# The last expert of layer 0 added by TensorE, the latents of layer 1 normed before its context, and layer 1's last slabs in halves

## The chip, the cores and the metric

The kernel runs on one core of a Trainium2 chip. A core has TensorE (PE, matrix products; its weight loads are shown apart as PEld), VectorE (DVE), ScalarE (ACT), GpSimd (POOL) and SyncE (SP), each with an order of its own; they meet through semaphores. Data lie in SBUF (128 partitions), products land in eight PSUM banks, and DMA queues carry data between HBM and SBUF. The metric is the device time of one execution in microseconds (us), the median of several; lower is better.

## The reference, cut to what matters

Two layers over 256 latent tokens and 256 context tokens of width 1024:

```python
for l in range(2):
    h = modulate(rms_norm(tokens, norm1_g[l]), shift, scale)          # latents and context, own modulation
    y = parallel_mixer(h, ...)                                        # one input projection; attention and HGRN2; output projection
    tokens = tokens + gate * y                                        # layer 1: latents only
    h2 = modulate(rms_norm(tokens, norm2_g[l]), shift2, scale2)
    tokens = tokens + gate2 * grouped_moe(h2, ...)                    # layer 1: latents only
return rms_norm(latents, final_g)

def grouped_moe(h, ...):                                              # 16 experts in 4 groups
    w = weights of the top 2 experts of the best group, per token
    return sum over e of w[:, e] * ((silu(h @ w_gate[e]) * (h @ w_up[e])) @ w_down[e])     # 1024 -> 512 -> 1024
```

All is float32, and a float32 product runs as two passes on PE, each with a record of its own in the trace (fp32r operands, split into a high and a low part, as one).

## The kernel before, in words

The token stream xT is kept with features on partitions: 8 feature tiles (KT) of 128, by 512 tokens; columns 0 to 255 are the context ("segment 0"), 256 to 511 the latents ("segment 1"). Weights stream through SBUF slabs of 2 MB. There is no scheduler: the order on each engine is the order of the code in that engine's block, and each engine waits on semaphores that count others' steps. So a step that stands early in an engine's block holds up all that is behind it there.

**Layer 0's experts** (dealt_experts). Every expert has 96 places, into which its tokens are dealt: 64 "near", 32 "rest". For each expert e, POOL gathers the rows of its tokens from token_table, PE turns them (L1185), and multiplies with gate and up: hidden_near (L1203, 64 places) and hidden_rest (L1214, 32). ACT applies silu, DVE multiplies into f_acts (L3101, L3109), PE turns it (turn_act, L1222), ACT copies f_turned, and PE multiplies with the down slab (down: L1232 near, L1239 rest). ACT copies the result to y_out, and SP stores it to expert_table in HBM (store_y, L1719 and L1721; the last expert's at L1768, its near half from ACT's queue). The hidden products of e + 1 stand before turn_act and down of e, which covers ACT and DVE. SP refills a slab when its products are over: gate and up at up_over, down (L1711) at down_over, in a fixed order per e, with the stores behind.

**join_tokens.** When all 16 experts are stored, POOL gathers for each of four blocks of 128 tokens the two rows of its two experts (tok_rows, L2512). ACT scales the first by its share (L2277), DVE adds the second times its share (L3129, "join"), PE turns the block (L1302), DVE adds it, times the modulation, to xT (L3137). Blocks 0 and 1 are context, 2 and 3 latents. PE multiplies ones meanwhile (L681, idle_products, read by nobody).

**Layer 1's first norm.** ACT squares xT (L2283), POOL adds squares of two tiles for six pairs (L2518), PE sums over features by one-column products (L1272), ACT takes the root (L2293), DVE its reciprocal, PE spreads it over partitions (L1285); DVE multiplies (normed, L2595, both segments at once), ACT modulates (hT, L1890, once per segment). normed has two buffers, so DVE waits for ACT's tile k - 2. Then PE makes the latents' queries (L823); ACT and DVE split hT into early_hi (L1943) and early_lo (L2637), the weights into near_hi (L1921) and ring_lo (L2655), and PE makes eight chunks of keys and gates for both segments, 24 passes each (L836, L840, L843).

**Layer 0's second norm** uses the same L2595 and L1890 ahead of the router.

**Layer 1's experts** (narrow_experts) take all 256 latents' chosen places, 64 per expert: gate L1472 and up L1473, turn L1485, down L1496, scatter of pairs of experts L1508 and L1512 (weights pair_hi and pair_lo, DVE, L3257 and L3267). SP loads each slab whole (L1641), in the order GATE e, UP e, DOWN e - 1, as slabs come free.

## Time and profile before

| what | us |
|---|---|
| median of three runs | 1462.76 (1461.70 to 1464.13) |
| profiled execution, its own time | 1461.11 |
| its span, first to last instruction | 1459.3 |
| PE busy / DVE / ACT / POOL in the span | 1400.1 / 694.5 / 527.2 / 157.1 |
| mean granted PE clock, share of full speed | 0.990 |
| last product of layer 0's experts to end of layer 1's first chunk | 836.7 to 894.2 |
| layer 0's second norm, first to last hT on ACT | 531.5 to 539.5 |
| layer 1's last expert, first gate product to the kernel's last product of experts | 1425.5 to 1449.7 |

Busy shares are averages over stages with different limits. What a stage is worth is read from what ends its waits last: a row of a timeline gives the start in us, the duration, engine and line, output and inputs, shapes, how many instructions were grouped, and in brackets how long the engine stood idle before and what released it. "issue" is a wait for nothing that the profile shows.

### The profile page before, as it was taken

What the parts mean: (1) busy time and instruction counts of PE and PEld (TensorE: products, weight loads), DVE (VectorE), ACT (ScalarE), POOL (GpSimd) and SP (SyncE); (2) the same over time, 40 slices, a digit from 0 to 9 for tenths busy, and PEclk for the clock granted to TensorE, in tenths of its full rate; (3) what the DMA queues carried; (4) which work ended last, traced back from release to release, by engine and by line L of the source; (5) the groups of instructions that cost most, each with busy time, mean ns of one, the idle gap of its engine ahead of it and who ended that gap; (6) DMA issues with size and microseconds to landing.
All of it is one profiled execution on the core that took longest, in us unless ns stands there. A gap on an engine that the chain in (4) does not pass through costs nothing. (4 is left out here: it accounts for less than half of the span.)

```text
span 1459.3 us, 20788 instructions
## 1 busy us (share of the span) xinstructions
PE 1400.1 (96%) x8454; PEld 899.4 (62%) x8454; DVE 694.5 (48%) x1201; ACT 527.2 (36%) x955; POOL 157.1 (11%) x163
## 2 busy tenths in 40 slices
PE   4999999999999999999999989999998998999997
PEld 2886667646888864444444378876856996344433
DVE  4477986475834442000000034976775774223223
ACT  5554452357233341111111136554346553112112
POOL 0007970000000001000000030074000000000000
PEclk9999999999999999999999979999999999999998
DMA  9762104671131758999999591120677756999993
GB/s 369 241 159 87 58 1 173 233 286 59 58 115 58 288 206 303 390 393 394 404 406 414 200 351 62 57 101 16 220 256 274 289 231 241 398 429 429 429 429 152
DMA packets 102952, 352.37 MB, mean 241 GB/s; under 512 B 23104, under 2 KB 26304, under 8 KB 88000
## 3 DMA queue, kind: packets, MB, share of 16 engines
q1 hardware_dynamic: 99136, 338.09, 60.4%
q0 software_dynamic: 2976, 10.49, 2.1%
q10 hardware_dynamic: 736, 2.36, 0.4%
q8 instruction: 71, 1.16, 0.3%
q14 instruction: 33, 0.27, 0.1%
HBM read 341.48 MB, written 13.63 MB: 243 GB/s over the span
## 5 line engine op out<-in xcount | busy, mean ns | idle before, releaser
L1472 PE MATMUL bank<-narrow_slab,picked 128*64 128x512 f32 x256 | 114.9, 602 | 3.7 <-issue 3.5
L1473 PE MATMUL bank<-narrow_slab,picked 128*64 128x512 f32 x256 | 115.0, 603 | 0.0
L1203 PE MATMUL bank<-slab,feed 128*64 128x512 f32 x512 | 113.4, 595 | 0.3 <-ACT feed L2227 0.3
L865 PE MATMUL bank<-hT,ring 128*128 128x512 f32 (+1 forms) x256 | 102.8, 539 | 0.0
L3101 DVE TENSOR_TENSOR f_acts<-bank,f_silu 64x512 f32<-64x512 f32 x16 | 11.1, 694 | 186.4 <-ACT f_silu L2233 186.4
L1203 PEld LDWEIGHTS bank<-slab,feed 128*64 128x64 f32 x512 | 35.8, 137 | 70.2 <-issue 70.2
L1472 PEld LDWEIGHTS bank<-narrow_slab,picked 128*64 128x64 f32 x256 | 34.1, 138 | 69.4 <-issue 68.0
L2500 POOL DMA_INDIRECT feed_rows<-token_table,slot_token x16 | 14.6, 913 | 551.5 <-DVE slot_token L3033 345.1
L3280 DVE TENSOR_TENSOR hidden<-bank,gated 64x512 f32<-64x512 f32 x16 | 17.4, 1085 | 109.4 <-ACT gated L2375 109.4
L865 PEld LDWEIGHTS bank<-hT,ring 128*128 128x128 f32 x256 | 45.9, 191 | 32.0 <-issue 30.6
L1232 PE MATMUL bank<-slab,f_turned 128*64 128x512 f32 x256 | 58.5, 598 | 0.6 <-issue 0.6
L1214 PE MATMUL bank<-slab,feed 128*32 128x256 f32 x1024 | 58.6, 380 | 0.0
L889 PEld LDWEIGHTS bank<-pair 128*128 128x128 f32 x384 | 47.1, 192 | 17.9 <-DVE pair L2739 11.2
L1496 PE MATMUL bank<-narrow_slab,hiddenT 128*64 128x512 f32 x256 | 57.8, 592 | 0.0
L2477 POOL TENSOR_TENSOR pair<-pf 128x512 f32<-128x512 f32 (+1 forms) x32 | 32.2, 1006 | 216.2 <-DVE pb L2702 205.8
L889 PE MATMUL bank<-pair 128*128 128x128 f32 x384 | 49.0, 277 | 3.0 <-DVE pair L2739 3.0
L2077 ACT ACTIVATE gsig<-bank 128x512 f32<-128x512 f32 (+1 forms) x32 | 15.8, 492 | 99.2 <-PE bank L1010 99.1
L2023 ACT ACTIVATE pair<-pair 128x1024 f32<-128x1024 f32 (+1 forms) x32 | 27.0, 843 | 59.8 <-POOL pair L2478 59.8
L2233 ACT ACTIVATE f_silu<-bank 64x512 f32<-64x512 f32 x16 | 9.5, 591 | 105.2 <-PE bank L1203 105.2
L2375 ACT ACTIVATE gated<-bank 64x512 f32<-64x512 f32 x16 | 9.4, 589 | 100.9 <-PE bank L1473 100.9
L1214 PEld LDWEIGHTS bank<-slab,feed 128*32 128x32 f32 x1024 | 31.6, 110 | 20.4
L2161 ACT ACTIVATE probs<-bank,narow 128x512 f32<-128x512 f32 (+1 forms) x48 | 29.4, 615 | 33.3 <-DVE narow L2892 33.2
(421 smaller groups left out, 3022.4 us busy)
## 6 DMA issues: line engine op xcount, KB each, us to landing
ring<-in_w_in SPq DMA_DIRECT2D x23, 2048.0 KB, 9.8
ring<-in_w_ada SPq DMA_DIRECT2D x16, 2048.0 KB, 11.2
slab<-in_w_gate SPq DMA_DIRECT2D x16, 2048.0 KB, 15.2
slab<-in_w_up SPq DMA_DIRECT2D x16, 2048.0 KB, 18.8
slab<-in_w_down SPq DMA_DIRECT2D x16, 2048.0 KB, 19.7
narrow_slab<-in_w_gate SPq DMA_DIRECT2D x16, 2048.0 KB, 15.3
narrow_slab<-in_w_up SPq DMA_DIRECT2D x15, 2048.0 KB, 20.8
narrow_slab<-in_w_down SPq DMA_DIRECT2D x15, 2048.0 KB, 24.3
```

What stands on the lines that cost most here:

```text
L865: mm = T.matmul(beside[0][:, a:TOK], w[:, k, c * P:(c + 1) * P], hT[:, k, a:TOK], start=(k == 0), stop=(k == KT - 1))
L889: mm = T.matmul(o[:, (2 * i + b) * P:(2 * i + b + 1) * P], left, right, start=True, stop=True)
L1203: mm = T.matmul(bank[e % 2][NEAR * kind:NEAR * (kind + 1), :], feed[e % 2][:, k, 0:NEAR], w[kind][:, k, :], start=(k == 0), stop=(k == KT ...
L1214: mm = T.matmul(bank[4][REST * c:REST * (c + 1), a:a + SEG], feed[e % 2][:, k, NEAR:DEALT], w[c // 2][:, k, c % 2 * SEG:(c % 2 + 1) * SEG] ...
L1232: mm = T.matmul(bank[6][NEAR * half:NEAR * (half + 1), :], f_turned[:, k * NEAR:(k + 1) * NEAR], w[:, k, half * 512:(half + 1) * 512], sta ...
L1472: T.matmul(bank[0][0:64, :], x, gate[:, k, :], start=(k == 0), stop=(k == KT - 1))
L1473: mm = T.matmul(bank[0][64:128, :], x, up[:, k, :], start=(k == 0), stop=(k == KT - 1))
L1496: mm = T.matmul(bank[3][64 * half:64 * half + 64, :], hiddenT[:, k, :], w[:, k, half * 512:(half + 1) * 512], start=(k == 0), stop=(k == 3))
L2023: S.activation(e[:, 0], e[:, 0], ACT.Exp)
L2161: S.activation(probs[at][:, 0:nk], result(("S", l, n))[:, 0:nk], ACT.Exp, bias=narow[:, at, 0:1], accum_out=narow[:, at, 1:2]).then_inc(se ...
L2477: G.tensor_tensor((stays, moves)[way][0], mid, left, ALU.subtract)
L3280: V.tensor_tensor(dealt(hidden[64:128, :], 4), in_turn(bank[0][64:128, :], 4), in_turn(gated[64:128, :], 4), ALU.mult) .then_inc(sem["hidd ...
```

## The change

- **Layer 0's last expert (15) is not stored and gathered.** After expert 4, DVE writes late_hot (hot_rows: for each token and place, the token's weight if it has that place at expert 15, 8 operations). PE turns it (turn_late), DVE copies it out as late_spread (2 copies). From y_out of expert 15, PE adds weights times rows straight into the banks that hold the turned rows (scatter_last): the latents into banks 0 to 3, later the context into banks 4 to 7. 8 products have 64 places on their rows, 8 have 32. The gathers cover experts 0 to 14, and wait for those alone; two small DVE operations zero the share of expert 15 in them.
- **Order.** Down of 14 stands ahead of hidden of 15. The latents' blocks 2 and 3 are joined first, turned around down_rest of 15, and added to xT by DVE (8 tiles), then the scattered 8 tiles once more. The context's blocks are turned by products with the identity (turn_joined) between the latents' squares, spread and norm; its squares are made by POOL (5 tiles) and DVE (3), and its norm follows the latents' one. hT, early_hi and early_lo are made per segment.
- **Down slabs.** At e = 12 SP loads DOWN 14 ahead of GATE 15 and UP 15. Layer 1's ring loads follow the gathers.
- **Layer 0's second norm.** ACT modulates the context, POOL the latents; the router's products wait for both.
- **Layer 1's last slabs.** GATE 15 and UP 15 are loaded in halves in turn, and PE waits for the first halves, then at k = 4 for the rest. The last pair_hi is made by ACT, and the table for the roots is loaded earlier.

Core of the diff:

```diff
+            def scatter_last(sg):
+
+                home = 0 if sg else 4
+                cols = slice(sg * SEG, (sg + 1) * SEG)
+                out = lambda d: bank[home + d // 2][:, d % 2 * SEG:(d % 2 + 1) * SEG]
+                pe.wait_ge(sem["late_kept"], 2)
+                pe.wait_ge(sem["y_kept"], 2 * N_EXPERTS - 1)
+                for d in range(4):
+                    for half in range(2):
+                        n = 4 * half + d
+                        if sg and d % 2 == 0:
+                            pe.wait_ge(sem["tok_added"], 2 * (n // 2) + 2)
+                        T.matmul(out(n), y_out[1][NEAR * half:NEAR * (half + 1), d * P:(d + 1) * P],
+                                 late_spread[NEAR * half:NEAR * (half + 1), 0, cols],
+                                 start=(sg == 1 and d % 2 == 0), stop=False)
+                pe.wait_ge(sem["y_kept"], 2 * N_EXPERTS)
+                for j in range(2):
+                    for c in range(4):
+                        mm = T.matmul(out(2 * c + j), y_out[1][REST * c:REST * (c + 1), 512 + j * P:512 + (j + 1) * P],
+                                      late_spread[REST * c:REST * (c + 1), 1, cols], start=False, stop=(j == 1))
+                        if j:
+                            mm.then_inc(sem["late_scattered"], 1)
...
+                    if k == 2:
+                        join_squares(0)
+                    if k == 3:
+                        spread_segment(0)
...
+                    def turn_late():
+
+                        pe.wait_ge(sem["row_of_ready"], 2)
+                        for part in range(2):
+                            pe.wait_ge(sem[("feed_high", "feed_low")[part]], N_EXPERTS)
+                            for t in range(4):
+                                mm = T.transpose(bank[2 + part][:, t * P:(t + 1) * P], late_hot[:, t, part, :], ident)
+                            mm.then_inc(sem["tok_turned"], 1)
+
+                    def latents_late():
+
+                        pe.wait_ge(sem["act_made"], 2 * N_EXPERTS)
+                        pe.wait_ge(sem["late_kept"], 2)
+                        for t in JOIN_ORDER[:2]:
+                            if t == JOIN_ORDER[1]:
+                                down_rest(LAST)
+                            pe.wait_ge(sem["tok_joined"], t - 1)
+                            for d in range(KT):
+                                c = d % 2 * SEG + t % 2 * P
+                                mm = T.transpose(bank[d // 2][:, c:c + P], tok_rows[0][:, t, d * P:(d + 1) * P], ident)
+                            mm.then_inc(sem["tok_turned"], 1)
+                        scatter_last(1)
...
+                    turn_act(LAST - 1)
+                    turn_late()
+                    down_near(LAST - 1)
+                    down_rest(LAST - 1)
+                    pe.wait_ge(sem["crowd_ready"], 1)
+                    crowded = pe.value_load(crowd_int[0:1, 0:1])
+                    hidden_near(LAST)
+                    hidden_rest(LAST)
+                    pe.wait_ge(sem["late_kept"], 2)
+                    idle_products(bank[3][:, 0:P], 4)
+                    turn_act(LAST)
+                    idle_products(bank[3][:, 0:P], 3)
+                    down_near(LAST)
+                    with pe.If(crowded > dealt_first[0]):
+                        latents_late()
...
-                    for t in range(4):
-                        if t:
-                            idle_products(bank[7][:, P:2 * P], 2)
-                        if t == 3:
-                            add_squares(0, range(2))
-                        pe.wait_ge(sem["tok_joined"], t + 1)
-                        for d in range(KT):
-                            c = d % 2 * SEG + t % 2 * P
-                            mm = T.transpose(bank[t // 2 * 4 + d // 2][:, c:c + P], tok_rows[0][:, t, d * P:(d + 1) * P], ident)
-                        mm.then_inc(sem["tok_turned"], 1)
...
+                    context_turned(3, 0)
+                    join_squares(1)
+                    context_turned(5, 1, range(4))
+                    spread_segment(1)
+                    context_turned(5, 1, range(4, KT))
+                    scatter_last(0)
...
+                        if e == LAST - 3:
+                            refill(e, DOWN, "down_over", 2 * e + 2)
...
+                        if late in HALVED and part == UP:
+                            e, kind = LATE_ORDER[m - 1 - len(FIRST)]
+                            name, k = spent_by[l][kind]
+                            sp.wait_ge(*total(2, None, name, e, k))
+                            for half in range(2):
+                                fill_first(m - 1, half)
+                                fill_first(m, half)
+                            continue
...
-                    pe.wait_ge(*total(1, None, "x_added", phases[1][1] - 1, 4))
-                    idle_products(bank[7][:, P:2 * P], 40)
-                    join_tokens()
...
-                    for sg in range(1 if lo else 0, 2):
+                    act.wait_ge(sem["normed_ready"], normed_before(count) + k + 1)
+                    for sg in range(1 if lo else 0, 1 if count == 1 else 2):
...
+                for k in range(KT):
+                    pool.wait_ge(sem["normed_ready"], KT + k + 1)
+                    G.tensor_scalar(hT[:, k, SEG:TOK], normed[:, k % 2, SEG:TOK], gain2[:, 0, k, 0:1], mod[:, 0, 3 * KT + k, 0:1],
+                                    ALU.mult, ALU.add).then_inc(sem["latents_modulated"], 1)
...
+                    def hot_rows():
+
+                        for t in range(4):
+                            for part, (first, size, copies) in enumerate(((0, NEAR, 2), (NEAR, REST, 4))):
+                                op = V.tensor_scalar(late_hot[:, t, part, :].rearrange("p (a n) -> p a n", a=copies),
+                                                     iota[:, first:first + size].unsqueeze(1).to_broadcast([P, copies, size]),
+                                                     place[:, t, LAST:N_EXPERTS], weight[:, t, LAST:N_EXPERTS],
+                                                     ALU.is_equal, ALU.mult)
+                        op.then_inc(sem["row_of_ready"], 1)
...
+                        for n, t in enumerate(JOIN_ORDER[:2]):
+                            join_rows(t, n)
+                        dve.wait_ge(sem["tok_turned"], 4)
+                        for d in range(KT):
+                            add_joined(1, d)
+                        join_rows(JOIN_ORDER[2], 2)
+                        for d in range(KT):
+                            dve.wait_ge(sem["late_scattered"], d // 2 + 1)
+                            add_joined(1, d)
...
-                        keep_high(None, N_EXPERTS - 2, 1, 1)
...
```

PE at the end of layer 0's experts, before: down of 14 (slab2), turn_act and down of 15 (slab4), then the branch that skips the overflow phase.

```order
L1232 MATMUL bank6<-slab2_248,f_turned_270 64x512 [waits y_kept,act_kept,slot_full2]
L1232 MATMUL bank6<-slab2_248,f_turned_270 64x512 x7
L1239 MATMUL bank7<-slab2_248,f_turned_270 32x256 [waits y_kept]
L1239 MATMUL bank7<-slab2_248,f_turned_270 32x256 x15
L1222 MATMUL bank5<-const_53,f_acts_269 128x64 [waits act_kept,act_made]
L1222 MATMUL bank5<-const_53,f_acts_269 128x64 x5
L1232 MATMUL bank6<-slab4_250,f_turned_270 64x512 [waits y_kept,act_kept,slot_full4]
L1232 MATMUL bank6<-slab4_250,f_turned_270 64x512 x7
L1239 MATMUL bank7<-slab4_250,f_turned_270 32x256 [waits y_kept]
L1239 MATMUL bank7<-slab4_250,f_turned_270 32x256 x15
L1571 TENSOR_LOAD crowd_int_69 [waits crowd_ready]
L1572 COMPARE_AND_BRANCH
```

The same place now, from turn_act of 14 on; late_hot are the weights' places, slab1 and slab3 up and gate of expert 15.

```order
L1311 MATMUL bank5<-const_53,f_acts_269 128x64 [waits act_kept,act_made]
L1311 MATMUL bank5<-const_53,f_acts_269 128x64 x5
L1342 MATMUL bank2<-const_53,late_hot_279 128x128 [waits feed_high,row_of_ready]
L1342 MATMUL bank2<-const_53,late_hot_279 128x128 x3
L1342 MATMUL bank3<-const_53,late_hot_279 128x128 [waits feed_low]
L1342 MATMUL bank3<-const_53,late_hot_279 128x128 x3
L1321 MATMUL bank6<-slab2_248,f_turned_270 64x512 [waits y_kept,act_kept,slot_full2]
L1321 MATMUL bank6<-slab2_248,f_turned_270 64x512 x7
L1332 MATMUL bank7<-slab2_248,f_turned_270 32x256 [waits y_kept,slot_full2]
L1332 MATMUL bank7<-slab2_248,f_turned_270 32x256 x15
L1375 TENSOR_LOAD crowd_int_69 [waits crowd_ready]
L1292 MATMUL bank1<-slab1_247,feed1_258 64x512 [waits act_made,feed_high,slot_full3,slot_full1]
```

Down of 14 moved ahead of hidden of 15, with turn_late and the register load; the branch comes behind down_near of 15.

ACT at the start of layer 1, before: squares, roots per segment, then hT of tile after tile for both segments.

```order
L2277 ACTIVATE tok_rows0_277<-tok_rows0_277,share_275 128x1024 [waits tok_there3]
L2283 ACTIVATE square_late_255<-xT_49 128x256 [waits tok_added] x12
L2293 ACTIVATE token_std_74<-bank0,epsv_72 128x2 [waits normed_ready,psum_ready]
L2283 ACTIVATE square_late_255<-xT_49 128x256 [waits tok_added] x4
L2293 ACTIVATE token_std_74<-bank1,epsv_72 128x2 [waits normed_ready,psum_ready]
L1890 ACTIVATE hT_50<-normed_119,mod_60,gain1_61 128x256 [waits normed_ready]
L1890 ACTIVATE hT_50<-normed_119,mod_60,gain1_61 128x256
```

And now, from the last of the scalings on.

```order
L2441 ACTIVATE tok_rows0_277<-tok_rows0_277,share_275 128x1024 [waits tok_there1]
L2435 ACTIVATE square_late_255<-xT_49 128x256 [waits tok_added] x8
L2018 ACTIVATE token_std_74<-bank0,epsv_72 128x2 [waits normed_ready,psum_ready]
L2000 ACTIVATE hT_50<-normed_119,mod_60,gain1_61 128x256 [waits normed_ready] x8
L2070 ACTIVATE early_hi_125<-hT_50 128x256 [waits h_ready] x8
L2037 ACTIVATE near_hi0_127<-ring_51 128x1024 [waits slot_full0]
L2037 ACTIVATE near_hi1_128<-ring_51 128x1024
L2018 ACTIVATE token_std_74<-bank0,epsv_72 128x2 [waits normed_ready,side_ready]
L2076 ACTIVATE hT_50<-normed_119,mod_60,gain1_61 128x256 [waits normed_ready]
L2079 ACTIVATE early_hi_125<-hT_50 128x256 [waits h_ready]
```

Squares, root and hT of the latents moved ahead of everything of the context, whose squares left ACT; the context's root stands behind early_hi and near_hi.

SP's last expert loads of layer 1, before; narrow_slab8 and 6 take GATE 15 and UP 15.

```order
L1641 DMA narrow_slab5_242<-in_w_down 128x4096 [waits halves_done]
L1641 DMA narrow_slab8_245<-in_w_gate 128x4096 [waits hidden_done]
L1641 DMA narrow_slab6_243<-in_w_up 128x4096 [waits hidden_done]
L1641 DMA narrow_slab7_244<-in_w_down 128x4096 [waits halves_done]
L1641 DMA narrow_slab0_237<-in_w_down 128x4096 [waits hidden_done]
```

And now, where 128x2048 is half a slab.

```order
L1738 DMA narrow_slab5_242<-in_w_down 128x4096 [waits halves_done]
L1738 DMA narrow_slab8_245<-in_w_gate 128x2048 [waits hidden_done]
L1738 DMA narrow_slab6_243<-in_w_up 128x2048
L1738 DMA narrow_slab8_245<-in_w_gate 128x2048
L1738 DMA narrow_slab6_243<-in_w_up 128x2048
L1738 DMA narrow_slab7_244<-in_w_down 128x4096 [waits halves_done]
L1738 DMA narrow_slab0_237<-in_w_down 128x4096 [waits hidden_done]
```

The whole loads of GATE 15 and UP 15 became four halves in turn; the down loads behind them stay.

## Rows read from the trace of the kernel before

**Rows 1.** Timeline of PE, 834 to 895: start, us, engine, line, operation, shapes, count, idle before.

```profile
834.81 1.93 PE L1239 MATMUL bank<-slab,f_turned 128*32 128x256 f32 x32
840.68 11.67 PE L681 MATMUL bank<-const 128*128 128x128 f32 x80 [3.93 <-issue]
...
860.83 0.58 PE L1272 MATMUL bank<-const,square_late 128*128 128x1 f32 x4 [1.69 <-POOL square_late L2518]
861.26 1.07 PE L1302 MATMUL bank<-const,tok_rows 128*128 128x128 f32 x8
...
864.65 5.25 PE L1272 MATMUL bank<-const,square_late 128*128 128x1 f32 x24 [0.26 <-POOL square_late L2518]
...
874.57 14.08 PE L823 MATMUL bank<-hT,ring 128*128 128x256 f32 x64 [0.70 <-ACT hT L1890]
...
892.16 2.02 PE L843 MATMUL bank<-early_hi,ring_lo 128*128 128x512 f32 x8
```

**Rows 2.** Timelines of SP, POOL, ACT and DVE around the same place.

```profile
837.22 1.94 SPq L1768 DMA_DIRECT2D expert_table<-y_out  x4
...
841.67 0.95 POOL L2512 DMA_INDIRECT tok_rows<-expert_table,row_of  x1 [67.18 <-issue]
...
850.17 1.15 ACT L2277 ACTIVATE tok_rows<-tok_rows,share 128x1024 f32<-128x1024 f32 x1 [12.98 <-DMA tok_rows<-expert_table,row_of]
...
873.43 7.97 ACT L1890 ACTIVATE hT<-normed,mod,gain 128x256 f32<-128x256 f32 x16 [3.23 <-DVE normed L2595]
881.30 4.25 ACT L1943 ACTIVATE early_hi<-hT 128x512 fp32r<-128x512 f32 x8
885.46 1.99 ACT L1921 ACTIVATE near_hi<-ring 128x1024 fp32r<-128x1024 f32 x2
...
821.20 0.69 DVE L3101 TENSOR_TENSOR f_acts<-bank,f_silu 64x512 f32<-64x512 f32 x1 [12.45 <-ACT f_silu L2233]
...
858.82 1.28 DVE L3129 SCALAR_TENSOR_TENSOR tok_rows<-tok_rows,share,tok_rows 128x1024 f32<-128x1024 f32 x1
...
862.37 3.23 DVE L3137 SCALAR_TENSOR_TENSOR xT<-bank,mod,xT 128x256 f32<-128x256 f32 x8 [0.31 <-PE bank L1302]
```

**Rows 3.** Windows: length, busy time of PE, PEld, DVE, ACT, POOL, granted clock, DMA, GB/s.

```profile
864.00:873.00 9.00, 8.74 (x40) 8.59 (x41) 2.13 (x8) 2.31 (x8) 1.23 (x2) 0.50 1.05 388
```

**Rows 4.** Timeline of ACT in layer 0's second norm.

```profile
531.52 7.97 ACT L1890 ACTIVATE hT<-normed,mod,gain 128x256 f32<-128x256 f32 x16 [2.18 <-DVE normed L2595]
```

**Rows 5.** Timeline of PE, layer 1's last expert.

```profile
1425.49 0.61 PE L1472 MATMUL bank<-narrow_slab,picked 128*64 128x512 f32 x1 [2.62 <-issue]
...
1426.54 1.06 PE L1472 MATMUL bank<-narrow_slab,picked 128*64 128x512 f32 x1
...
1434.08 3.63 PE L1496 MATMUL bank<-narrow_slab,hiddenT 128*64 128x512 f32 x16
...
1447.84 1.06 PE L1508 MATMUL bank<-pair_hi,spread 128*128 128x256 f32 x4
```

**Rows 6.** Timeline of SP's queue, the loads of UP 15, DOWN 14 and DOWN 15.

```profile
1393.47 0.43 SPq L1641 DMA_DIRECT2D narrow_slab<-in_w_up  x1
1396.54 8.87 SPq L1641 DMA_DIRECT2D narrow_slab<-in_w_down  x2
```

**Rows 7.** DMA issues of 1393 to 1396 and 1396 to 1404: size, us to landing.

```profile
narrow_slab<-in_w_up SPq DMA_DIRECT2D x1, 2048.0 KB, 31.8
...
narrow_slab<-in_w_down SPq DMA_DIRECT2D x1, 2048.0 KB, 33.6
```

**Rows 8.** Timeline of PE in layer 0's attention: products with 64 rows.

```profile
300.72 0.70 PE L955 MATMUL bank<-nak,naq 64*128 64x256 f32 x4
```

**Rows 9.** Timeline of POOL, the pairs of squares.

```profile
859.48 1.20 POOL L2518 TENSOR_TENSOR square_late<-square_late 128x256 f32<-128x256 f32 x1 [7.88 <-ACT square_late L2283]
861.02 2.29 POOL L2518 TENSOR_TENSOR square_late<-square_late 128x256 f32<-128x256 f32 x3 [0.34 <-ACT square_late L2283]
```

**Rows 10.** The page's DMA issues: stores of y by SP, median us to landing.

```profile
expert_table<-y_out SPq DMA_DIRECT2D x30, 128.0 KB, 16.1
```

566 lines of the change are left out of this document (354 added, 212 removed).

## The prediction

> **What bounds the kernel now.** TensorE (PE) is the busiest engine by far, so I looked for the stretches in which it stands or runs work that nobody reads: first its timeline, then at each gap the engine that released it, then the windows with the granted clock.
>
> Three stretches bear on this change. The **seam** between layer 0's experts and layer 1 [rows 1]: the last expert's last product ends at 834.81 + 1.93 = 836.74; then 3.93 us of nothing, 11.67 us of filler products (L681), and the first chunk of layer 1's keys ends at 892.16 + 2.02 = 894.18. That is 57.4 us, of which only the queries (L823, 14.08 us) and one chunk (about 5.9 us) are large PE work. Its chain runs over the others [rows 2]: the stores of the last y (837.22, 1.94), the first gather on POOL at 841.67, its rows at ACT at 850.17, that is 8.5 us later, joins of 1.28 us and adds of 3.23 / 8 = 0.40 us on DVE. Then come squares, norm, and both segments' 16 hT on ACT (7.97 us). The clock falls in it [rows 3]: granted 0.50 (the 1.2 GHz level) in 864 to 873, where PE does little but one-column products (L1272).
>
> Second, **layer 0's second norm** goes at ACT's pace [rows 4]: 16 in 7.97 us, 0.996 us for each of 8 feature tiles. Third, **layer 1's last expert** waits 2.62 us, to 1425.49, for its weights [rows 5]: UP 15 is issued at 1393.47 [rows 6] and lands 31.8 us later, at 1425.3, and DOWN 14 lands at 1396.54 + 33.6 = 1430.1 [rows 7].
>
> **The seam, step by step.** Times are those of the clock of before; first with PE at the upper level.
>
> 1. Down of expert 14 now stands ahead of hidden of 15. Beside the same products PE gets 8 turnings of the weights' places (8 turnings take 0.95 us, 861.26 to 862.17 without its drain) [rows 1], a register load (1.0) and some 1.4 us of fillers while ACT and DVE make the last activations, which down of 14 covered before. So the last down_near ends near 838.1, where it ended at 834.8. The load and the branch lay in the 3.93 us of idle time of before, together with eight semaphore steps [rows 1]; bounds for both together are 0 and 3.9 us. I take 2.0, half, since the steps are gone from this place; 0.4 would gain 1.6 us, 3.9 lose 1.9.
> 2. Branch (to 839.1), turnings of block 2, down_rest, turnings of block 3: 842.9.
> 3. Gathers no longer wait for the last expert. y of 14 is kept by 820.8, stored by 822.8; with the 2.5 us that lay between the end of the stores and the first gather (839.16 to 841.67) POOL starts at 825.3, and with 8.5 us ACT gets rows at 833.8. Blocks 2 and 3 are joined near 839 [rows 2]. PE wants them at 839.1 and 841.9: about 3 us of slack for the second.
> 4. DVE adds the latents (8 of 0.40, to 846.2). PE scatters the last expert from y itself: 16 products, 32 passes, 8 products with 64 rows and 8 with 32. Four 64-row passes of 256 columns take 0.70 us with their drain [rows 8]; full passes take 14.08 / 64 = 0.22 each, 0.88 for four [rows 1]. So two run side by side (0.11 each) with some 0.2 on top, and I let four do so for 32 rows: 16 x 0.11 + 16 x 0.055 + 2 x 0.2 = 3.0 us. Bounds 2.6 (no change) and 32 x 0.22 = 7.0 (nothing side by side). I take 3.0, the row being of the same form. Latents complete: 851.2.
> 5. Context block 0 is turned by products (16 passes of 0.12: 2.1 us, where transposes took 0.95). The latents' squares on PE are 32 one-column passes: 7.0 us by the 0.22 of the lower level (5.25 / 24); at the upper one between 0.43 / 4 = 0.11 and 0.145 [rows 1], I take 4.3. Squares end at 855.3, std, reciprocal and spread at 856.9, first hT near 857.9, where the first of before is at 873.43 [rows 2].
> 6. PE turns the rest of the context, scatters it (3.0), starts queries: 863.7. The context's squares, another 4.3 us, end at 868.1. ACT is behind them in its own queue: 8 hT, spaced by DVE's context adds between them (864.6), 8 early_hi of about 0.33 (half the columns of a row of 0.53), two near_hi of 1.0 [rows 2], so the context's std stands at 869.2, its spread at 870.
> 7. DVE norms the context, per tile 0.41 + 0.35 + 0.35 (halves of rows of 0.69 and 0.61) and one ring_lo of 1.2: 879. Remaining passes of the first chunk: 883.8.
>
> So 894.2 - 883.8 = **10.4 us** at the upper level. Against that stands the clock: steps 5 to 7 hold two runs of one-column products and a thin stretch, 875 to 880, the kind in which it fell before [rows 3]. Low through the first squares alone costs 3.0 by the same steps, low through both 7.1, low from 851 to 882 12.3. I take 3.4, nearest to the first, because before both runs stood next to each other and here turnings, scatter and queries lie between. Seam: **10.4 - 3.4 = 7.0**.
>
> **Ports on POOL.** POOL's square at 859.48 took 1.20 us while DVE's join (858.82 to 860.10, both inputs in SBUF) ran, and three later ones 2.29, 0.76 each, beside adds whose second input is PSUM [rows 2, 9]. The Trainium skill's page "SBUF — State Buffer", section "Who interferes with whom", says that a DVE instruction with two SBUF inputs and a GpSimd one that reads SBUF shut each other out, and one with a single SBUF input doesn't. The rows agree; by it the second norm's DVE (one input in PSUM) is undisturbed, while POOL's five context squares may meet DVE's three: 0.8 to 1.6 us on a step that ends 1.1 before ACT is ready, so 0.5 us at most.
>
> **Second norm of layer 0.** POOL takes the latents' half. ACT's 0.5 and DVE's 0.69 per tile remain; POOL's one-input operation has no row, its two-input one 0.76 to 1.20 [rows 9]. Pace 0.8 instead of 0.996: 8 x 0.19 = **1.5** gained; at 0.69 it is 2.4, at 1.20 a loss of 1.6. I take 0.8, a little over the undisturbed row.
>
> **Tail.** GATE and UP of 15 come in interleaved halves. 2 MB take 1430.1 - 1425.3 = 4.8 us, so both first halves lie there at 1420.5, both wholes at 1425.3. Hidden can start where its wait began, 1422.9, and needs the second halves half of its 7.0 us later, at 1426.4. Without the wait its passes should not stretch to 1.06 either, as those after 1426.54 did, and it ends near 1430. Down of 14 then waits for DOWN 14, 1430.1, and starts there instead of 1434.08 [rows 5, 7]: **3.9**. Two bounds: 2 (the halves' smaller pieces land late), 4.2. pair_hi moved to ACT counts nothing: PE's products follow one another at 1447.84 without a wait [rows 5].
>
> **At no cost.** The 8 hot-row operations and two copies lie in DVE's 12.45 us of waiting per expert [rows 2]; without it they would cost some 3 us. DOWN 14 first on SP pushes GATE 15 and UP 15 back by one slab, 4.8 us, while hidden of 15 itself moves back by the down and the turnings of step 1, over 6 us; without that cover it costs the difference. Layer 1's first ring load moves from 839 to 842, and is needed at 861.
>
> **Sum.** 7.0 + 1.5 + 3.9 = 12.4 us. The profiled execution took 1461.11, so 1448.7; the median of before is 1.65 above it: **1450.4 us**.
>
> On the scatter, the Trainium skill ("TensorEngine Tiling (Array Packing)", "Key Properties" and "Theoretical Speedup") gives up to two times for 64 rows and four for 32, and a drain at each change of mode. Without drains this estimate is 2.6 us instead of 3.0, 0.7 us for both scatters.
>
> **Rivals.** (a) The clock stays at 1.2 GHz from the first squares to the end of the context's norm. For it: before, it came back only after 873, with dense work [rows 3]; against: queries and scatter between. 12.3 for 3.4: 12.4 - 8.9 = 3.5, **1459.3**. (b) The gathers start late. The stores of 14 lie behind DOWN 15 on SP's queue; the median of the y stores in the loaded stage is 16.1 us [rows 10]. Landing 9.2 us later costs 9.2 less the slack, 6.6: **1457.0**. Against: DOWN 15 should be through by 823. (c) The halves bring nothing, because the four pieces land together: 12.4 - 3.9 = 8.5, **1454.3**. (d) Slower: in the scatters nothing runs side by side, since all 32 passes add to few banks, and the clock falls with them: 32 x 0.43 = 13.8 us each, twice, and low until 882. By the steps the chunk then ends at 907.2, the seam loses 13.0, and 1.5 + 3.9 - 13.0 = -7.6: **1470.4**. It decides once a scatter exceeds about 9 us. (e) The new order doesn't do what it says: PE reaches the same places at the same time, because DVE's double adds (16 x 0.40 and a join) and ACT's queue take what the gathers gave: about **1462.8**.
>
> **Chances.** As summed 0.59, its own range 1446 (the clock never falls, 3.4 better, and POOL at its best, 0.9) to 1455; (a) 0.12, (b) 0.08, (c) 0.10, (d) 0.08, (e) 0.03. A measurement of this kernel can tell about 0.2%, 2.9 us, from no change. Within that, 1459.8 to 1465.7, lie (e) and under half of (a): 0.08; slower is (d), 0.08; faster 0.84. The range leaves out (d), (e), the upper half of (a) and the low tail: 1445 to 1459.5.
>
> **What would show it.** Right: rows at ACT before 836; the latents' first hT near 858; the first chunk's end between 882 and 890; hidden of 15 at 1422.9; a norm-2 pace of 0.8. Wrong: granted clock 0.50 beyond 860; a scatter over 5 us; the wait before block 2's turnings over 3 us; a wait for DOWN 14 past 1431.

## The result, and the profile after

The changed kernel took 1449.35 us (median of five, 1448.36 to 1453.55) against 1462.61 for the kernel before: ratio 0.9913, 95% interval 0.9898 to 0.9929. Forecast were 1450.4 and a range of 1445 to 1459.5. The span went from 1459.3 to 1446.7 us. Line numbers from here on are those of the changed kernel.

The seam, in the timeline of PE (start, us, engine, line, operation, shapes, count, idle before), answers to [rows 1]:

```profile
811.62 1.09 PE L1342 MATMUL bank<-const,late_hot 128*128 128x128 f32 x8
812.64 3.65 PE L1321 MATMUL bank<-slab,f_turned 128*64 128x512 f32 x16
...
831.16 3.66 PE L1321 MATMUL bank<-slab,f_turned 128*64 128x512 f32 x16
837.04 1.06 PE L1355 MATMUL bank<-const,tok_rows 128*128 128x128 f32 x8 [2.22 <-issue]
838.03 1.94 PE L1332 MATMUL bank<-slab,f_turned 128*32 128x256 f32 x32
839.90 1.09 PE L1355 MATMUL bank<-const,tok_rows 128*128 128x128 f32 x8
842.05 0.67 PE L821 MATMUL bank<-late_spread,y_out 64*128 64x256 f32 x2 [1.06 <-DVE xT L2785]
843.53 1.99 PE L821 MATMUL bank<-late_spread,y_out 64*128 64x256 f32 x14 [0.81 <-DVE xT L2785]
...
848.87 3.63 PE L849 MATMUL bank<-const,square_late 128*128 128x1 f32 x32
852.36 1.55 PE L806 MATMUL bank<-const,tok_rows 128*128 128x128 f32 x8
...
856.39 2.00 PE L821 MATMUL bank<-late_spread,y_out 64*128 64x256 f32 x16
858.32 1.15 PE L827 MATMUL bank<-late_spread,y_out 32*128 32x256 f32 x16
859.40 5.45 PE L881 MATMUL bank<-hT,ring 128*128 128x256 f32 x24
864.68 3.63 PE L849 MATMUL bank<-const,square_late 128*128 128x1 f32 x32
...
880.01 0.50 PE L923 MATMUL bank<-early_hi,near_hi 128*128 128x512 f32 x1 [0.44 <-ACT early_hi L2079]
...
884.05 1.98 PE L923 MATMUL bank<-early_hi,near_hi 128*128 128x512 f32 x8
```

Where 3.93 us of standing and 11.67 us of fillers were, PE now stands 2.22 us, waits twice more for DVE (1.06 and 0.81 us), and otherwise has something to multiply. The second chunk starts at 884.05, where it was 894.03.

The other engines there (SP, POOL, ACT, DVE), for [rows 2]:

```profile
819.42 1.87 SPq L1868 DMA_DIRECT2D expert_table<-y_out  x4
...
826.62 0.95 POOL L2660 DMA_INDIRECT tok_rows<-expert_table,row_of  x1 [54.48 <-issue]
...
833.49 1.15 ACT L2441 ACTIVATE tok_rows<-tok_rows,share 128x1024 f32<-128x1024 f32 x1 [2.60 <-DMA tok_rows<-expert_table,row_of]
...
868.35 0.26 ACT L2018 ACTIVATE token_std<-bank,epsv 128x2 f32<-128x2 f32 x1 [0.90 <-PE bank L849]
...
834.68 1.28 DVE L2779 SCALAR_TENSOR_TENSOR tok_rows<-tok_rows,share,tok_rows 128x1024 f32<-128x1024 f32 x1 [5.01 <-ACT tok_rows L2441]
```

The gathers start at 826.62, 13 us before PE's last down_rest ends (838.03 + 1.94 = 839.97), not after it. The row at 868.35 matters below: ACT waits 0.90 us for PE's context squares. The last row is the join of block 2, done at 835.96, 1.1 us before PE turns it.

Windows of the same place (length, busy PE, PEld, DVE, ACT, POOL, granted clock, DMA, GB/s), for [rows 3]:

```profile
846.00:852.00 6.00, 5.59 (x57) 5.22 (x50) 4.51 (x9) 3.16 (x8) 0.00 (x0) 1.00 1.05 396
852.00:858.00 6.00, 6.00 (x39) 5.64 (x40) 1.76 (x5) 2.45 (x5) 0.00 (x0) 0.72 1.05 387
858.00:864.00 6.00, 6.00 (x41) 4.82 (x38) 4.51 (x13) 3.30 (x8) 3.06 (x5) 1.00 1.05 387
```

The second norm, ACT, POOL and DVE, for [rows 4], and the tail on PE, for [rows 5]:

```profile
531.63 1.20 ACT L2000 ACTIVATE hT<-normed,mod,gain 128x256 f32<-128x256 f32 x2 [2.18 <-DVE normed L2746]
533.08 1.20 ACT L2000 ACTIVATE hT<-normed,mod,gain 128x256 f32<-128x256 f32 x2 [0.25 <-DVE normed L2746]
...
531.70 1.15 POOL L2640 TENSOR_SCALAR hT<-normed,gain,mod 128x256 f32<-128x256 f32 x2 [324.45 <-DVE normed L2746]
...
532.36 1.29 DVE L2746 TENSOR_TENSOR normed<-xT,bank 128x512 f32<-128x512 f32 x2 [0.17 <-POOL hT L2640]
```

```profile
1412.85 0.64 PE L1579 MATMUL bank<-narrow_slab,picked 128*64 128x512 f32 x1
...
1420.26 3.65 PE L1603 MATMUL bank<-narrow_slab,hiddenT 128*64 128x512 f32 x16 [0.33 <-DMA narrow_slab<-in_w_down]
...
1437.06 3.43 PE L692 MATMUL bank<-const 128*128 128x256 f32 x8 [1.27 <-PEq L487]
1440.33 1.91 PE L1704 MATMUL bank<-const,y_rows 128*128 128x128 f32 x16
```

ACT starts two tiles each 533.08 - 531.63 = 1.45 us, so one each 0.72, and POOL needs 1.15 / 2 = 0.58. The last expert's hidden products follow without a wait, and down of 14 waits 0.33 us for its slab. The last two rows show something not foreseen: eight filler passes before the last turnings took 3.43 us; they took 1.97 before.

So I cut each trace at the same instructions. In us:

| stage, from and to | before | after | again (e12) | e5: norm and halves alone | e13: seam alone |
|---|---|---|---|---|---|
| norm: first normed to the first turning of hT behind the router's products | 9.73 | 7.38 | 7.39 | 7.40 | 9.72 |
| experts of layer 0, to the end of down 13 | 272.93 | 272.82 | 273.95 | 274.01 | 273.01 |
| seam, to the second chunk of layer 1 | 80.58 | 72.95 | 75.60 | 80.73 | 78.50 |
| on to down of 13, layer 1 | 523.69 | 523.71 | 522.76 | 522.40 | 524.74 |
| tail, down 13 to down 14 | 16.36 | 12.50 | 12.52 | 12.49 | 16.34 |
| end, down 14 to the last turnings | 18.83 | 20.07 | 17.71 | 18.00 | 18.68 |

Each stage begins where the one above it ends. The norm (-2.35) repeats: 7.37 to 7.40 us in every trace in which POOL modulates. So does the tail (-3.86): 12.40 to 12.53 us in every trace with halves. The seam does not: 7.6 us gained in one execution, 5.0 in another.

### The profile page after: what moved, and what is told of

It reads as the page before. It is cut to its first block and busy times, and to the rows that moved or that the text cites. A ratio compares the mean times of both kernels' runs of the same rounds, so it can differ in the third digit from the quotient of the medians.

```text
span 1446.7 us, 20895 instructions
## 1 busy us (share of the span) xinstructions
PE 1394.5 (96%) x8480; PEld 894.3 (62%) x8480; DVE 702.9 (49%) x1238; ACT 524.4 (36%) x949; POOL 160.3 (11%) x170
## 5 line engine op out<-in xcount | busy, mean ns | idle before, releaser
L1579 PE MATMUL bank<-narrow_slab,picked 128*64 128x512 f32 x256 | 113.3, 595 | 1.2 <-issue 0.9
L1580 PE MATMUL bank<-narrow_slab,picked 128*64 128x512 f32 x256 | 113.3, 596 | 0.0
L1603 PEld LDWEIGHTS bank<-narrow_slab,hiddenT 128*64 128x64 f32 x256 | 18.4, 137 | 36.7 <-issue 35.5
```

The lines of the kernel that those rows point to most:

```text
L1579: T.matmul(bank[0][0:64, :], x, gate[:, k, :], start=(k == 0), stop=(k == KT - 1))
L1580: mm = T.matmul(bank[0][64:128, :], x, up[:, k, :], start=(k == 0), stop=(k == KT - 1))
L1603: mm = T.matmul(bank[3][64 * half:64 * half + 64, :], hiddenT[:, k, :], w[:, k, half * 512:(half + 1) * 512], start=(k == 0), stop=(k == 3))
```

## The experiments

Each is the changed kernel with one edit, unless it says otherwise. Ratios are to the kernel before on the same chip. The changed kernel has 0.9913 in its first runs, and 0.9915 in a second set (e12) beside e6, e11 and e13; on the chips of the other experiments it wasn't run.

**The parts.** First the halves:

```diff
-    HALVED = (N_EXPERTS - 1,)
+    HALVED = ()
```

> The changed kernel with GATE and UP of layer 1's last expert loaded whole again, gate first; all else stays. My theory: the halves alone carry the tail's gain, so down of expert 14 in layer 1 starts 3.8 us later against the issue of its slab than in the changed kernel, and the run takes about 1453 us if the rest follows, or 1452 if the fillers before the last turnings run faster, as they did in the kernel before (1.97 us for 8 passes, 3.43 in the changed kernel). Rival: the tail was gained because the seam moved everything 10 us earlier against the queue; then the time stays at 1449.4.

Measured 1454.53 us, 0.9948 (0.9930 to 0.9966). PE's rows around the last expert:

```profile
1414.43 0.46 PE L1592 MATMUL bank<-const,hidden 64*128 64x64 f32 x4
1417.46 1.09 PE L1579 MATMUL bank<-narrow_slab,picked 128*64 128x512 f32 x1 [2.57 <-issue]
```

The wait of 2.57 us is back, the first pass takes 1.09, and from down 13 to down 14 it is 17.47 us, 5.0 more than with halves. The halves carry the tail; the rival is out. The 17.47 is also 1.1 more than before the change (16.36): the granted clock was 0.57 over 1416 to 1424 here, and 0.57 over 1426 to 1430 only in the kernel before.

The norm:

```diff
-                    for sg in range(1 if lo else 0, 1 if count == 1 else 2):
+                    for sg in range(1 if lo else 0, 2):
...
-                    G.tensor_scalar(hT[:, k, SEG:TOK], normed[:, k % 2, SEG:TOK], gain2[:, 0, k, 0:1], mod[:, 0, 3 * KT + k, 0:1],
-                                    ALU.mult, ALU.add).then_inc(sem["latents_modulated"], 1)
```

> The changed kernel with layer 0's second norm modulated by ACT alone, both segments, as before; POOL's eight operations are gone. Theory: the norm's pace goes from 0.72 us per tile back to 0.98 and the time rises by 2.3 to 2.5 us, to about 1451.8. Rival: the norm's gain is given back further on (slabs of the first experts land no earlier), then the first expert's products start at the same time and the run stays at 1449.4.

Measured 1456.11 us, 0.9954 (0.9937 to 0.9972). The stage took 9.73 us again, 2.35 more. The time rose by more than that, with a wide spread (1448.4 to 1459.0); in the profiled execution the seam took 76.15 us and the experts 274.21, 3.2 and 1.4 more than in the first trace of the changed kernel. Those two also differ between executions of one kernel (e12), so only the 2.35 is put down to the edit. What the rest of the rise is stays open: the expectation of 1451.8 was missed, and the ten times were spread over more than 10 us.

The order of the down slabs:

```diff
-                        if e == LAST - 3:
-                            refill(e, DOWN, "down_over", 2 * e + 2)
...
-                            if e != LAST - 3:
-                                refill(e, DOWN, "down_over", 2 * e + 2)
+                            refill(e, DOWN, "down_over", 2 * e + 2)
```

> The changed kernel with the down slab of expert 14 loaded behind GATE 15 and UP 15 again. In the changed kernel its first product runs at 812.64. Theory: the slab then lands some 9 us later than now, near 814 to 816, and PE waits 1 to 3 us in front of down of 14: 1450.5 to 1452. Rival: it lands in time anyway, since in the kernel before it landed at 816.0, 2.35 us of which are gone with the second norm, that is 813.7: 1 us at most, within what can be told from 1449.4.

Measured 1451.34 us, 0.9936 (0.9914 to 0.9958), and no wait in front of down of 14:

```profile
811.70 1.09 PE L1342 MATMUL bank<-const,late_hot 128*128 128x128 f32 x8
812.72 3.65 PE L1321 MATMUL bank<-slab,f_turned 128*64 128x512 f32 x16
```

The rival holds: the slab is there anyway, and this part of the change does nothing that can be measured in the time. It does move something: with the old order the first gather began 2.9 us after the last store was issued (820.90 to 823.79), against 5.3 in the changed kernel's first trace. The block then lay joined at 833.33, and PE still turned it at 837.97, behind a standing of 3.06 us. So gathers earlier than the changed kernel's gained nothing in this trace.

Norm and halves put into the kernel before (the same two edits, the other way round):

> The kernel before with two parts of the change alone: POOL modulates the latents in layer 0's second norm, and GATE and UP of layer 1's last expert come in halves. The seam stays as it was. Theory: 2.4 us from the norm and 3.8 from the tail, less at most 1.4 where the fillers before the last turnings run at 1.2 GHz, so 4.8 to 6.2 us under the kernel before; what is left to the changed kernel, 6.5 to 8 us, is the seam's. Rival: the seam gives less than it seems and these two carry nearly all: 9 us or more under the kernel before.

Measured 1455.21 us, 0.9951 (0.9936 to 0.9966): some 6.2 us under the kernel before, the upper end of what was expected, with the seam at its old 80.7 us.

The seam alone (e1's and e2's edits together):

> The changed kernel with the other two parts undone: ACT alone modulates layer 0's second norm, GATE and UP of layer 1's last expert come whole. What is left of the change is the seam (last expert added by PE, latents first) and the order of the down slabs. Theory: the parts add up, so the seam alone lies 5 to 7.6 us under the kernel before, where norm and halves alone lay 6.2 under it. Rival: the parts help each other, and the seam alone gives under 4 us.

Measured 1456.75 us, 0.9958 (0.9940 to 0.9976), 6.3 us under the kernel before. 0.9951 and 0.9958 leave 0.9909 if the parts add up, and the changed kernel has 0.9913. Within the intervals they do. Taken out one at a time they fit less well: the ratio rises by 0.0035 without the halves (e1), by 0.0041 without the norm (e2), and by only 0.0045 without both (e13). The difference, 0.0031, is about what the intervals of the four allow together, so whether the parts help each other a little stays open. The profiled execution of e13 had a long seam (78.50; a standing of 3.25 us before block 2 and four stretches at the lower clock).

**What the seam's gain hangs on.** One wait more on POOL before the gathers:

```diff
+                pool.wait_ge(sem["act_kept"], N_EXPERTS)
                 for t in JOIN_ORDER:
```

> The changed kernel with one wait more on POOL: the first gather also waits for the last expert's turned activations (830.9 in the changed kernel's trace, where the gathers begin at 826.6). Theory: the early gathers bring the seam's gain and have about 1 us of slack (joined 839.3, PE there at 839.9), so the blocks are joined 4.3 us later and the time rises by 3 to 4 us, to 1452.5 to 1453.5. Rival: the seam's end is set by PE's own work and the split norm, and 4 us are taken up by waits on the way (1.06 and 0.81 us before the scatter): under 2 us.

Measured 1456.39 us, 0.9967 (0.9952 to 0.9983). The first gather began 20.4 us after the turning of the weights' places (15.0 in the changed kernel). The join of block 2 on DVE, and then PE, show what that cost:

```profile
842.44 1.29 DVE L2780 SCALAR_TENSOR_TENSOR tok_rows<-tok_rows,share,tok_rows 128x1024 f32<-128x1024 f32 x1 [11.00 <-ACT tok_rows L2441]
...
843.88 1.94 PE L1355 MATMUL bank<-const,tok_rows 128*128 128x128 f32 x8 [7.28 <-DVE tok_rows L2780]
845.75 3.16 PE L1332 MATMUL bank<-slab,f_turned 128*32 128x256 f32 x32
```

```profile
837.00:844.00 7.00, 0.12 (x1) 0.15 (x2) 1.29 (x1) 1.43 (x2) 4.89 (x6) 0.82 0.93 325
844.00:849.00 5.00, 5.00 (x41) 2.89 (x42) 1.28 (x1) 2.51 (x4) 0.00 (x0) 0.57 0.77 307
```

Counted from that turning, the gathers were 5.4 us later. Their rows took 0.6 us longer to come, so block 2 was joined 6.0 us later, at 843.73. The slack of 1.1 us was there and took up its part: PE waited 5.1 us more. Then came a clock of 0.57, at which eight turnings take 1.94 instead of 1.06 and down_rest 3.16 instead of 1.94. The seam took 80.1 us, as long as before the change. Against the seam of e12 (75.6) that is 4.5 us more, near the 3 to 4 expected; against the first trace 7.1. The times rose by some 7 us, twice what was expected; one trace doesn't settle why.

So the seam's gain hangs on the early gathers: with them 5.4 us later the kernel took 1456.39 us, and on the same chip norm and halves without any of the seam took 1455.21. It isn't shown what the other pieces of the seam (the latents first, the context's norm behind theirs) give by themselves, since no run takes out one of them alone.

**Who ends the first chunk.** The context's spread ahead of the fourth query tile:

```diff
                     if k == 2:
                         join_squares(0)
-                    if k == 3:
                         spread_segment(0)
```

> The changed kernel with the context's spread put right behind its squares on PE, ahead of the fourth of the latents' query tiles (in the changed kernel it stands 1.8 us behind them, 0.9 us after its reciprocal). Theory now: PE itself is the bound of this stretch, since the queries took 1.76 us per tile and not the 0.88 that the prediction put in; the chain of the context's norm starts 1.1 us earlier but PE waits about 0.65 for it, so under 0.5 us changes. Rival, the prediction's step 7: the norm's chain over DVE and ACT is the bound, and the first chunk ends 1.1 us earlier, counted from the start of the squares.

Measured 1449.78 us, 0.9911 (0.9888 to 0.9933): no change. From the start of the context's squares to the second chunk it is 20.61 us; in e12, on the same chip and with the same stretches at the lower clock, 20.62. PE's rows:

```profile
867.76 3.63 PE L849 MATMUL bank<-const,square_late 128*128 128x1 f32 x32
872.03 0.73 PE L859 MATMUL bank<-const,token_rstd 128*128 128x128 f32 x4 [0.64 <-DVE token_rstd L2812]
872.55 10.48 PE L881 MATMUL bank<-hT,ring 128*128 128x256 f32 x40
882.68 2.17 PE L922 MATMUL bank<-early_hi,near_hi 128*128 128x512 f32 x8
```

PE now waits 0.64 us for the reciprocal, and then never again: the 0.45 us that it waited for early_hi in e12 are gone. What the chain gains PE gives back. This stretch is bound by PE and by the chain almost alike.

**The standing behind down_near.** The branch moved ahead of the last turn_act, inside both of its arms:

```diff
+                        pe.wait_ge(sem["late_kept"], 2)
+                        turn_act(LAST)
+                        idle_products(bank[3][:, 0:P], 3)
+                        down_near(LAST)
...
-                    pe.wait_ge(sem["late_kept"], 2)
-                    idle_products(bank[3][:, 0:P], 4)
-                    turn_act(LAST)
-                    idle_products(bank[3][:, 0:P], 3)
-                    down_near(LAST)
                     with pe.If(crowded > dealt_first[0]):
                         latents_late()
```

> The changed kernel with PE's branch moved ahead of the last turn_act, into the place of the first four fillers (1.16 us there, 2.22 us of standing behind down_near in the changed kernel). Theory: the branch's 2.2 us lie in part beside ACT's and DVE's work on the last activations, PE turns block 2 about 1.1 us earlier, and then block 3 waits for its join (839.3): 0.5 to 1 us less, 1448.4 to 1448.9. Rival: the standing is not the branch's but the wait for the joined block 2, and stays behind down_near: no change.

Measured 1450.83 us, 0.9918 (0.9894 to 0.9942): no change.

```profile
832.67 0.87 PE L1311 MATMUL bank<-const,f_acts 64*128 64x64 f32 x6 [3.63 <-issue]
833.47 1.65 PE L692 MATMUL bank<-const 128*128 128x128 f32 x6
835.05 5.76 PE L1321 MATMUL bank<-slab,f_turned 128*64 128x512 f32 x16
840.74 1.09 PE L1358 MATMUL bank<-const,tok_rows 128*128 128x128 f32 x8
```

The standing went with the branch, so it is the branch's and not a wait for block 2. (e3 says the same: there block 2 was joined 4.6 us before PE turned it, and PE still stood 3.06 us.) But it grew to 3.63 us, and behind it the granted clock was 0.60 over 833 to 841, so the last down took 5.76 us instead of 3.66. Whether the fillers ahead of it had kept the clock up isn't told apart from the standing itself.

**The clock.** Two filler products among the latents' squares:

```diff
                 for k in range(KT):
+                    if sg == 1 and k in (4, 6):
+                        idle_products(bank[1][:, 0:SEG], 1)
```

> The changed kernel with two filler products of 256 columns among the latents' 32 one-column passes (0.9 us more for PE). In the changed kernel the granted clock is 1.00 up to 852, 0.72 over 852 to 858, and the context's second turning and the spread take 1.7 us more than at the upper level. Theory: it is the one-column stretch that lets the clock fall; with the fillers it stays at 1.00 and PE reaches the queries some 0.8 us earlier, 1448.5. Rival: the clock falls here whatever PE runs (it also fell at other places in other executions), and the fillers cost their 0.9 us: 1450.2.

Measured 1453.34 us, 0.9938 (0.9914 to 0.9963).

```profile
852.00:858.00 6.00, 6.00 (x39) 5.90 (x39) 1.53 (x3) 0.80 (x3) 0.00 (x0) 0.75 1.05 388
858.00:864.00 6.00, 6.00 (x44) 4.87 (x43) 1.59 (x4) 2.18 (x4) 0.00 (x0) 0.68 1.05 386
```

The clock fell in the same place and stayed down longer. So these two fillers don't hold it, and the theory's forecast is out. That the one-column passes have nothing to do with the fall isn't shown by this: the clock fell at the end of the latents' squares in all twelve traces of kernels with the new seam, this one included. The rival says nothing about why it was worse than 0.9 us, but the trace does in part. The clock was low for longer behind the context's squares too:

```profile
868.00:874.00 6.00, 6.00 (x41) 5.82 (x40) 3.09 (x9) 4.35 (x11) 0.26 (x1) 0.84 0.02 4
874.00:880.00 6.00, 6.00 (x20) 4.97 (x20) 1.78 (x6) 1.30 (x4) 0.00 (x0) 0.59 0.00 0
```

In e12 below it was back at 1.00 by 877. The seam took 79.34 us here, 3.7 more than in e12. Why both stretches were longer isn't shown.

No fillers before the last turnings:

```diff
-                idle_products(bank[0][:, 0:SEG], 4)
                 for b in range(4):
                     pe.wait_ge(sem["early_rows"], b // 2 + 1)
```

> The changed kernel without the four filler products ahead of the last turnings of the output rows. In the changed kernel they ran at 1.2 GHz, 3.43 us instead of 1.97, and ended 1.4 us after the first rows were there. Theory: the fillers themselves hold the end, and without them the turnings start 1.4 to 2 us earlier but run at the lower clock (16 transposes in about 3.6 us instead of 1.91), so that 0 to 1 us is left: 1448.4 to 1449.4. Rival: the turnings wait for DVE and ACT rows piece by piece, the lower clock costs them nothing, and the whole 1.3 us shows: 1448.1.

Measured 1450.22 us, 0.9921 (0.9901 to 0.9941).

```profile
1441.35 3.65 PE L1703 MATMUL bank<-const,y_rows 128*128 128x128 f32 x16 [2.53 <-DVE y_rows L3605]
```

The turnings start when their rows are there, and take 3.65 us at the lower clock. From the start of the last scatter's last row to their end it is 7.2 us, against 7.5 with fillers at the lower clock and 5.7 (e3) with fillers at the upper one. The theory held in this: little or nothing is to be had. Its forecast of 0 to 1 us less isn't told apart from no change.

Fillers in the waits of the last scatter (two products of 256 columns, one before pair_hi, one before pair_lo):

```diff
+                            if last and half == 0:
+                                idle_products(bank[1][:, 0:SEG], 1)
                             pe.wait_ge(*total(ph, i, "hi_kept", e, half + 1))
...
+                            if last and half == 0:
+                                idle_products(bank[1][:, 0:SEG], 1)
                             pe.wait_ge(*total(ph, i, "lo_kept", e, half + 1))
```

> The changed kernel with two filler products of 256 columns (0.9 us of PE) in the waits of the last scatter, 1.45 and 0.71 us in the changed kernel. There the clock fell to 0.50 over 1434 to 1438 and the last scatter's and filler passes took 3.2 us more than in executions in which it did not. Theory: PE's waits let the clock fall here, and with fillers in them it stays: 1.3 us less where it fell, nothing elsewhere. Rival: as with the fillers among the squares, it falls or not whatever stands there: no change, or 0.3 us more.

Measured 1450.60 us, 0.9914 (0.9889 to 0.9939). In its trace the clock was 1.00 from the tail to the end of the last turnings. It was so too in that of the unchanged kernel beside it (e12), so the trace can't tell the two apart; the time says no change.

The changed kernel once more:

> The changed kernel as it is, beside the three others on their chip. Theory: the places at which the clock falls differ from execution to execution of one kernel, so the stretch from the turning of the weights' places to the second chunk differs by 1 to 4 us from the 72.4 of the changed kernel's first trace, and the time lies at 1449 to 1451. Rival: the falls stand at fixed instructions, and the stages repeat within 0.3 us.

Measured 1450.44 us, 0.9915 (0.9892 to 0.9938). Windows of its seam:

```profile
844.00:849.00 5.00, 4.19 (x24) 2.88 (x26) 2.98 (x6) 1.15 (x1) 0.00 (x0) 0.66 0.72 239
849.00:855.00 6.00, 5.59 (x60) 5.21 (x52) 4.51 (x9) 3.16 (x8) 0.00 (x0) 1.00 1.06 392
855.00:859.00 4.00, 4.00 (x23) 4.00 (x23) 0.42 (x2) 0.26 (x1) 0.00 (x0) 0.57 1.05 387
...
873.00:877.00 4.00, 4.00 (x15) 3.41 (x15) 1.82 (x6) 1.45 (x3) 0.00 (x0) 0.66 0.00 0
```

Three falls, at the latents' scatter, behind the latents' squares and behind the context's; the first trace had the second alone. The same instructions take 2.65 us more. In nine executions (the first trace, e1 to e4, e6, e11 to e13; e3 moves one load and e6 one spread, the others leave this stage as the change has it) it took 72.95 to 78.50 us, 75.6 in the middle. Read in steps of 1 us, the granted clock goes with the length:

| stretches below full clock in the seam | seam, us |
|---|---|
| one | first trace 72.95 |
| two | e1 74.20, e4 74.73, e3 74.89 |
| three | e12 75.60, e6 75.74, e11 75.90, e2 76.15 |
| four | e13 78.50 |

So each costs about 1.4 us, an estimate from 72.95 with one and 75.6 to 76.2 with three. The fall at the end of the latents' squares is in all nine, one behind the context's in six; the others lie between the branch and the end of the latents' scatter, at different places. Both theory and rival are right in part: one fall stands at fixed instructions, the others don't. No version was found that beats the changed kernel.

## Why the prediction was right, and where it was not

**The sum** said 12.4 us; 13.3 were measured between the medians, 12.6 between the spans, and 12.6 between the medians of e12's set (1463.03 and 1450.44). That it came so near is in part luck: the first trace's seam is the shortest of nine, with the fewest stretches at the lower clock, and errors of both signs stand in the sum. Its three terms came out as follows.

**Seam: 7.0 forecast, 7.6 in the first trace, about 5.0 (80.58 - 75.6) in the middle of nine.** The mechanism stood: gathers beside the last expert, and no long run of fillers. e13 shows the seam's gain by itself (6.3 us), and e10 loses it by delaying the gathers. The last down_near of step 1 ended at 834.82, which is 837.2 on the clock of before (the seam now starts 2.35 us earlier, the norm's gain), for 838.1. The scatter of step 4 was on the mark: the context's 32 passes took 856.39 to 859.40, 3.0 us, with 0.12 us for a 64-row pass of 256 columns and 0.07 for a 32-row one. The Trainium skill's "Theoretical Speedup" ("TensorEngine Tiling (Array Packing)") makes it, as an estimate, 0.11 and 0.055 from the 0.22 of a full pass, and these rows come near to it. The squares took 3.5, not 4.3.

Three steps failed, in both directions:

- Step 6 has PE at 863.7 when three query tiles are done; by its own steps the scatter ends near 861. That is 0.88 us per tile. A tile is four products, so eight passes of the 0.22 that step 4 itself worked out, 1.76. The 24 passes took 5.45 us (L881). So the context's squares began 3.3 us later than written (864.68, which is 867.0 on the clock of before), 2.6 of it by the tiles, and it was PE that ended the context's sum and not ACT's queue: ACT waited 0.90 us for it. That step 7 then still ended near the right place in the first trace (884.05, which is 886.4 on the clock of before, for 883.8 + 3.4) is luck: the squares and the clock cost less than assumed.
- Step 3 put the first gather 2.5 us behind the end of the stores; it was 5.3 (819.42 + 1.87 = 821.29 to 826.62). The rows then came sooner, 6.9 us after and not 8.5. Of the slack of 3 us for the second block 0.6 was left (joined at 839.31, turned at 839.90), and 1.1 for the first. With the old order of the down slabs (e3) the 5.3 were 2.9; the prediction counted that order at nothing for the gathers. What delays the first gather isn't shown.
- The clock: 3.4 us were taken, nearest to 3.0 for a fall through the first squares alone. That fall came, in every trace, but each costs about 1.4 us, and there is one in the first trace and three in the middle one. Without any the seam would have gained about 9 us (an estimate, 80.58 - 72.95 + 1.4), where the steps had 10.4. So both parts of the term were too large, and in the first trace the smaller cost of the clock outweighed the rest.

The load and the branch of steps 1 and 2 were put at 1.0 us each. The load left no gap in PE's rows; behind the branch PE stood 2.22 us.

**Second norm: 1.5 forecast, 2.35 measured.** The direction and place were right, the size off: POOL's one-input operation takes 0.58 us, not 0.8, so the pace of 0.72 is DVE's own 0.64 (two in 1.29) and the 0.16 us for which it waits on POOL at each pair. The nearest row, a two-input operation of 0.76, was too dear a stand-in. The bound of 2.4 was what came.

**Tail: 3.9 forecast, 3.86 measured.** Each step can be read off: hidden right behind the turnings (1412.85), no pass of 1.06, and DOWN 14 as the next late thing (0.33 us of waiting at 1420.26). e1 shows that the halves do it. Part of the gain is the clock: before, it was 0.57 over 1426 to 1430, inside the last expert's hidden products.

**Not in the sum:** the end, 1.2 us longer in the first trace by the fillers at the lower clock, shorter in most others; it decides nothing. The down slabs' order was counted at nothing, and e3 finds nothing in the time.

**The rivals.** (a), a clock that stays down, came true in part, by stretches. (b), late gathers, is real as a mechanism: e10 prices a delay of 5.4 us at 4.5 of seam against the middle of the nine, 7.1 against the first trace, and of the 3 us of slack that spoke against it 0.6 to 1.1 was there. (c) and (d) fell: the halves work, the scatter's passes do run side by side. (e) fell with e13. On the ports of POOL and DVE: the operations of L2518 from which the prediction took 0.76 and 1.20 us are additions of two squares, not squares. The second norm's POOL operations repeat at 1.15 to 1.16 us for two beside DVE's. The five context squares took 3.43 us, 0.69 each, and ended at 863.55, before DVE's three began at 863.95; so the meeting that the prediction priced did not take place, and no run shows what it would cost.

## What to carry to other kernels

Where a stage ends with "store, gather, join", look for the last producer: if its share can be added by a product straight from where it lies, the gather can start one producer earlier, and the wait for it lies beside work. Before trusting a sum of passes, divide a row of the old trace by its passes once for every operation that is moved, not only for the new ones. And cut two traces at the same instructions before crediting a part: stages that repeat to 0.1 us and stages that wander by 3 us and more stood side by side here, the second kind with the number of stretches at the lower clock, and medians alone would have given the norm's edit 6 us.

## What the runs showed of the hardware

- The granted clock fell at the end of the latents' 32 one-column passes in all twelve traces with the new seam, and two fillers among them did not hold it (e7: 0.75 and 0.68 over 852 to 864). Other falls came in some executions of one kernel and not in others: one fall in the first seam, three in e12's. The two long standings of the experiments were followed by a low stretch (3.63 us in e8, then 0.60; 7.28 in e10, then 0.57). Standings of 2 to 3 us at the same place were followed by one in some traces (2.27 in e6) and not in others (3.06 in e3).
- PE stood 1.9 to 3.6 us behind a branch (1.87 in e1, 2.22 in the changed kernel, 3.06 in e3, 3.63 in e8, where it moved with the branch). What in the branch takes the time isn't shown.
- POOL modulates 128 x 256 floats with two per-partition scalars in 0.58 us; it multiplies a tile of that size by itself in 0.69, and added two of them in 0.76 in the kernel before.
